# A feed-forward whose gate/up pairs go by Strassen's scheme in a two-block network kernel

## The reference

```python
D_MODEL = 1024; SEQ = 512; DEPTH = 2; D_FF = 2816

def rms_norm(x, w):
    y = xf * lax.rsqrt(jnp.mean(xf * xf, axis=-1, keepdims=True) + NORM_EPS)
    return (y * w.astype(jnp.float32)).astype(x.dtype)

def swiglu_ffn(x, w_gate, w_up, w_down):
    return (jax.nn.silu(x @ w_gate) * (x @ w_up)) @ w_down

for l in range(DEPTH):
    x = x + 0.5 * swiglu_ffn(rms_norm(x, ffn1_norm_w[l]), ffn1_w_gate[l], ffn1_w_up[l], ffn1_w_down[l])
    x = x + hybrid_mixer(rms_norm(x, mix_norm_w[l]), ...)
    x = x + 0.5 * swiglu_ffn(rms_norm(x, ffn2_norm_w[l]), ffn2_w_gate[l], ffn2_w_up[l], ffn2_w_down[l])
```

## Time and profile before

| | us |
|---|---|
| median of 3 runs | 3319.2 (3318.94 to 3319.91) |
| span of the profiled execution | 3318.2 |
| TensorE busy | 3261.9 |
| VectorE busy | 1223.7 |
| ScalarE busy | 1229.1 |
| GpSimd busy | 1382.5 |

### The profile page before, as it was taken

One profiled execution on the slowest core, in us unless ns is written; L12 is line 12 of the kernel. 1 busy time (PEld: TensorE's weight loads), 2 busy tenths in 40 slices (PEclk: granted clock), 3 DMA queues, 4 the chain that ended last, 5 costly groups with the idle time before them and its releaser, 6 DMA issues.

```text
span 3318.2 us, 40330 instructions
## 1 busy us (share of the span) xinstructions
PE 3261.9 (98%) x16417; PEld 2646.5 (80%) x16417; DVE 1223.7 (37%) x2060; ACT 1229.1 (37%) x1830; POOL 1382.5 (42%) x614
## 2 busy tenths in 40 slices
PE   8999999999999999999999999999999999999998
PEld 6888877788888888877788887778866796878887
DVE  4220476432203220386432205743455434542211
ACT  4322445432314222445443314521366452343322
POOL 5444532354445444532354445553211242434442
PEclk9999999999999999999999999999999999999999
DMA  5332321233323332321233323238233432223332
...
DMA packets 470469, 305.99 MB, mean 92 GB/s; under 512 B 68840, under 2 KB 441944, under 8 KB 470284
## 3 DMA queue, kind: packets, MB, share of 16 engines
...
## 4 chain that ended last, share of the span: by engine, by line
PE 86%; DVE 9%; ACT 2%; DVEq 1%; issue 1%; DMA 0%; SPq 0%; POOL 0%; ACTq 0%
PE ps L545 37%; PE ps L563 13%; PE ps L3175 5%; PE ps L959 3%; PE ps L2852 3%; PE ps L1303 3%; PE ps L2497 3%; PE ps L1531 2%; PE ps L1311 2%; DVE h_lo L392 1%; PE ps L3153 1%; PE ps L798 1%; PE ps L2176 1%; PE ps L2864 1%; PE ps L2896 1%; PE ps L2874 1%
## 5 line engine op out<-in xcount | busy, mean ns | idle before, releaser
L179 POOL TENSOR_TENSOR w_lo<-w_raw,w_hi 128x1024 fp32r<-128x1024 f32 x518 | 1279.2, 2472 | 1891.1 <-ACT w_hi L171 1890.3
L171 ACT ACTIVATE w_hi<-w_raw 128x1024 fp32r<-128x1024 f32 x518 | 543.8, 1054 | 1001.7 <-PE ps L545 354.6
L545 PE MATMUL ps<-h_hi,w_hi 128*128 128x512 f32 x1952 | 768.1, 393 | 7.0 <-DVE h_lo L392 4.3
L545 PE MATMUL ps<-h_hi,w_lo 128*128 128x512 f32 x1952 | 760.4, 390 | 0.0
L545 PE MATMUL ps<-h_lo,w_hi 128*128 128x512 f32 x1952 | 760.3, 390 | 0.0
L545 PEld LDWEIGHTS ps<-h_hi,w_hi 128*128 128x128 f32 x1952 | 366.8, 188 | 89.9 <-issue 7.0
L545 PEld LDWEIGHTS ps<-h_lo,w_hi 128*128 128x128 f32 x1952 | 366.9, 188 | 78.2 <-issue 3.4
L545 PEld LDWEIGHTS ps<-h_hi,w_lo 128*128 128x128 f32 x1952 | 366.9, 188 | 77.1
L563 PE MATMUL ps<-a_hi,w_hi 128*128 128x512 f32 x640 | 249.0, 389 | 0.0
L563 PE MATMUL ps<-a_lo,w_hi 128*128 128x512 f32 x640 | 249.0, 389 | 0.0
L563 PE MATMUL ps<-a_hi,w_lo 128*128 128x512 f32 x640 | 249.0, 389 | 0.0
...
## 6 DMA issues: line engine op xcount, KB each, us to landing
w_raw<-in_w_in_dram SPq DMA_DIRECT2D x128, 512.0 KB, 3.8
...
```

The lines of the kernel that those rows point to most:

```text
L171: act.activation(self.hi[:, s, :, :], self.raw[:, s, :, :], ACT.Copy).then_inc(self.halved[s], 1)
L179: pool.tensor_tensor(self.lo[:, s, :, :], self.raw[:, s, :, :], self.hi[:, s, :, :].bitcast(F32), ALU.subtract)\
L545: mm = pe.matmul(out, w, (c.h_hi, c.h_lo)[low][:, k, :], start=(k == 0 and i == 0), stop=(k == KD - 1 and i == 2))
```

## The change

KF and the tiles stay. The first WHOLE = 2 pairs are made as before. For the other N = 20, the 1024 rows of weight are cut into two halves of 4 chunks, and the tokens into an early and a late half of 256. Gate and up of a pair are then a product of 2x2 blocks, which Strassen's scheme (in Winograd's form) makes with seven block products in place of eight: `first`, `second`, ... `seventh`, each 4 chunks x 3 passes = 12 matmuls of 256 columns.

The scheme needs sums of its operands. Once in a feed-forward, in its head, ScalarE makes a plain `h` (eight activations) and VectorE four sums of 128x1024 of it (`sum`, `s_plain`); ScalarE and VectorE split them into `s_hi` and `s_lo`, and the one called `sum` into the late half of `h_hi` and `h_lo`. Once in a pair, VectorE makes four sums of 128x512 of the raw weights (`pair_first`, two in `pair_second`, `pair_seventh`); ScalarE rounds them and one raw half (`pair_high`), and GpSimd makes three of the rests and that of the raw half (`pair_low`), VectorE the fourth (`second_low`). The up tile no longer goes through `high_to` and `low_to`; the gate tile does. A slot is loaded again only when the sums that read it are made as well (`read_too`).

Partial products are added while they leave PSUM: ScalarE copies the first (`keep`, 128x256), and VectorE adds (`m.second`, `m.third`, late and early up, late gate, each 128x256). TensorE waits for some of these before it adds the next product into the same bank. The products `a` of silu and up stay plain in `a_rows`; `a_hi` and `a_lo` are now rings of A_RING = 6 rows in the place of `s_hi` and `s_lo`, filled during the down product (`row_high`, `row_low`). The transposes of the last feed-forward use banks 3 and 7 (two in place of four), and the down product opens bank 3 first.

```diff
-def ffn(nc, c, acc, scale, g, finish=None, turns=None, late_sum=False):
+WHOLE = 2
...
+        self.a_hi = nc.alloc_sbuf_tensor_at(f"a_hi_{nc.next_id()}", [P, A_RING, SEQ], F32R, offset=s_at)
...
+        def row_high(act, j):
+            if j < KF:
+                act.wait_ge(c.product.sem, pb + j + 1)
+                if j >= A_RING:
+                    w.wait_used(act, t0 + 2 * KF + j - A_RING)
+                act.activation(m.a_hi[:, j % A_RING, :], m.a[:, j, :], ACT.Copy).then_inc(c.a_high.sem, 1)
...
+            def product(out, w_hi, w_lo, x_hi, x_lo, opens):
+                for k in range(KH):
+                    for i, (wt, x) in enumerate(((w_hi, x_hi), (w_hi, x_lo), (w_lo, x_hi))):
+                        mm = pe.matmul(out, wt[:, k, :], x(k), start=(opens and k == 0 and i == 0), stop=(k == KH - 1 and i == 2),
+                                       skip_group_check=True)
...
+            def sixth(n):
+                pe.wait_ge(c.second_low.sem, sb + n + 1)
+                product(bank(n, 1), m.t_hi[:, 0], m.t_lo[:, 0], of_mix(m.s_hi, 0), of_mix(m.s_lo, 0), True).then_inc(c.partial.sem, 1)
...
+            def seventh(n):
+                pe.wait_ge(*spread_at(n, SECOND))
+                pe.wait_ge(c.pair_low.sem, qb + 3 * n + 2)
+                product(bank(n, 1), m.t_hi[:, 1], m.t_lo[:, 1], of_mix(m.s_hi, 1), of_mix(m.s_lo, 1), False).then_inc(c.partial.sem, 1)
...
+            for n in range(N):
...
+                sixth(n)
...
+                fifth(n)
+                second(n)
+                seventh(n)
+                third(n)
+                if n < N - 1:
+                    first(n + 1)
+                fourth_product(n)
...
+            def pair_high(n):
+                t = up_tile(n)
+                act.wait_ge(c.pair_made.sem, tb + 4 * n + 1)
+                act.activation(high(t, 0), first_sum(n), ACT.Copy).then_inc(c.pair_high.sem, 1)
+                act.wait_ge(c.pair_made.sem, tb + 4 * n + 2)
+                act.activation(m.t_hi[:, 0], m.t_plain[:, 0], ACT.Copy).then_inc(c.pair_high.sem, 1)
+                w.wait_loaded(act, t)
+                act.activation(high(t, 1), raw(t, 1), ACT.Copy).then_inc(w.halved[t % SLOTS], 1)
+                f = fourth(n)
+                act.wait_ge(c.pair_made.sem, tb + 4 * n + 3)
+                act.activation(m.t_hi[:, f], m.t_plain[:, f], ACT.Copy).then_inc(c.pair_high.sem, 1)
+                act.wait_ge(c.pair_made.sem, tb + 4 * n + 4)
+                act.activation(m.t_hi[:, 1], m.t_plain[:, 1], ACT.Copy).then_inc(c.pair_high.sem, 1)
...
+            def keep(n):
+                act.wait_ge(c.partial.sem, xb + 1 + (5 * (n - 1) + NEXT1 if n else 0))
+                if n >= 2:
+                    act.wait_ge(*spread_at(n - 2, GATE2))
+                act.activation(m.first[:, n % 2, :], bank(n, 0), ACT.Copy).then_inc(c.first_kept.sem, 1)
...
+            for k in range(KD):
+                ins = act.activation(m.h[:, k, :], c.x_T[:, k, :], ACT.Copy, scale=c.gains[:, own, k:k + 1])
+            ins.then_inc(c.h_scaled.sem, 1)
...
+            def pair_low(n):
+                t = up_tile(n)
+                pool.wait_ge(c.pair_made.sem, tb + 4 * n + 2)
+                pool.wait_ge(c.pair_high.sem, jb + 4 * n + 1)
+                pool.tensor_tensor(low(t, 0), first_sum(n), high(t, 0).bitcast(F32), ALU.subtract).then_inc(c.pair_low.sem, 1)
+                pool.wait_ge(w.halved[t % SLOTS], t // SLOTS + 1)
+                pool.tensor_tensor(low(t, 1), raw(t, 1), high(t, 1).bitcast(F32), ALU.subtract).then_inc(w.split[t % SLOTS], 1)
+                for i, made in ((1, 4), (fourth(n), 3)):
+                    pool.wait_ge(c.pair_high.sem, jb + 4 * n + made)
+                    pool.tensor_tensor(m.t_lo[:, i], m.t_plain[:, i], m.t_hi[:, i].bitcast(F32), ALU.subtract).then_inc(c.pair_low.sem, 1)
...
+            def mix_low(i, made):
+                dve.wait_ge(c.mix_high.sem, ib + made)
+                dve.tensor_tensor(m.s_lo[:, i], m.s_plain[:, i], m.s_hi[:, i].bitcast(F32), ALU.subtract).then_inc(c.mix_low.sem, 1)
...
+            def pair_first(n):
...
+                dve.tensor_tensor(first_sum(n), raw(up_tile(n), 0), raw(gate_tile(n), 0), ALU.subtract).then_inc(c.pair_made.sem, 1)
+
+            def pair_second(n):
+                dve.drain()
+                dve.tensor_tensor(m.t_plain[:, 0], raw(up_tile(n), 1), first_sum(n), ALU.subtract).then_inc(c.pair_made.sem, 1)
+                dve.drain()
+                dve.tensor_tensor(m.t_plain[:, fourth(n)], raw(gate_tile(n), 1), m.t_plain[:, 0], ALU.subtract).then_inc(c.pair_made.sem, 1)
+
+            def pair_seventh(n):
+                t = up_tile(n)
+                dve.tensor_tensor(m.t_plain[:, 1], raw(t, 1), raw(t, 0), ALU.subtract).then_inc(c.pair_made.sem, 1)
+
+            def second_low(n):
+                dve.wait_ge(c.pair_high.sem, jb + 4 * n + 2)
+                dve.tensor_tensor(m.t_lo[:, 0], m.t_plain[:, 0], m.t_hi[:, 0].bitcast(F32), ALU.subtract).then_inc(c.second_low.sem, 1)
+
+            def second_gate(n):
+                p = (WHOLE + n) % 2
+                dve.wait_ge(*last_at(n))
+                dve.tensor_tensor(gt[:, p, LATE], bank(n, 1), m.first[:, n % 2, :], ALU.add)
+                dve.drain()
+                dve.tensor_tensor(gt[:, p, LATE], gt[:, p, LATE], c.rstd[:, LATE], ALU.mult).then_inc(c.spread.sem, 1)
...
+            dve.wait_ge(c.h_scaled.sem, c.h_scaled.n + 1)
+            dve.tensor_tensor(m.sum[:, :, :], m.h[:, 0:KH, LATE], m.h[:, KH:KD, LATE], ALU.add).then_inc(c.mix_made.sem, 1)
+            dve.drain()
+            dve.tensor_tensor(m.s_plain[:, 0], m.sum[:, :, :], m.h[:, 0:KH, EARLY], ALU.subtract).then_inc(c.mix_made.sem, 1)
+            dve.drain()
...
+            gate_whole(0)
+            mix_low(0, 1)
+            mix_low(2, 2)
+            mix_low(1, 3)
+            up_whole(0)
...
+            up_whole(1)
+            dve.wait_ge(c.mix_high.sem, ib + 4)
+            dve.tensor_tensor(c.h_lo[:, 0:KH, LATE], m.sum[:, :, :], c.h_hi[:, 0:KH, LATE].bitcast(F32), ALU.subtract)\
...
+            for n in range(N):
+                p = (WHOLE + n) % 2
+                if n:
+                    second_gate(n - 1)
+                if n < N - 1:
+                    pair_first(n + 1)
+                dve.wait_ge(*partial_at(n, SUM2))
+                dve.wait_ge(c.first_kept.sem, fb + n + 1)
+                dve.tensor_tensor(m.second, bank(n, 1), m.first[:, n % 2, :], ALU.add).then_inc(c.spread.sem, 1)
+                if n < N - 1:
+                    pair_second(n + 1)
+                dve.wait_ge(*partial_at(n, SUM5))
+                dve.tensor_tensor(m.third, bank(n, 2), m.first[:, n % 2, :], ALU.add).then_inc(c.spread.sem, 1)
+                if n < N - 1:
+                    second_low(n + 1)
+                multiply(WHOLE + n - 1)
+                w.wait_used(dve, gate_tile(n))
+                dve.tensor_tensor(gt[:, p, EARLY], bank(n, 0), c.rstd[:, EARLY], ALU.mult).then_inc(c.spread.sem, 1)
+                dve.wait_ge(*partial_at(n, SUM7))
+                dve.drain()
+                dve.tensor_tensor(up[:, p, LATE], bank(n, 1), m.third, ALU.add).then_inc(c.spread.sem, 1)
+                if n < N - 1:
+                    pair_seventh(n + 1)
+                w.wait_used(dve, up_tile(n))
+                dve.tensor_tensor(up[:, p, EARLY], bank(n, 2), m.second, ALU.add).then_inc(c.spread.sem, 1)
+                dve.drain()
+                dve.tensor_tensor(up[:, p, :], up[:, p, :], c.rstd[:, :], ALU.mult)
+            second_gate(N - 1)
...
+            def row_low(j):
+                dve.wait_ge(c.a_high.sem, hb + j + 1)
+                dve.tensor_tensor(m.a_lo[:, j % A_RING, :], m.a[:, j, :], m.a_hi[:, j % A_RING, :].bitcast(F32), ALU.subtract)\
...
-            for i in range(KF):
-                p = i % 2
...
+            for j in range(A_RING):
+                row_low(j)
```

More of the change, by code:

```diff
@@ L638, in ffn, with pairs_read @@
+def pairs_read(c, t0):
+    for n in range(KF - WHOLE):
+        t = t0 + 2 * (WHOLE + n)
+        c.w.read_too[t] = c.pair_made.at(4 * n + 3)
+        c.w.read_too[t + 1] = c.pair_made.at(4 * n + 4)
+def ffn(nc, c, acc, scale, own, g, finish=None, turns=None, late_sum=False):
     w = c.w
     a = c.arena
+    ps = c.ps
     t0 = w.take(3 * KF)
+    N = KF - WHOLE
     with a.scope():
-        a_hi, a_lo = a.sb("a_hi", [P, KF, SEQ], F32R), a.sb("a_lo", [P, KF, SEQ], F32R)
-        both = a.sb("both", [P, 4, SEQ])
@@ new lines, in bank, with raw, high, low @@
+        def bank(n, x):
+            return ps[:, (4, 0)[n % 2] + x, 0:HALF]
+        def raw(t, half):
+            return w.raw[:, t % SLOTS, KH * half:KH * half + KH, :]
+        def high(t, half):
+            return w.hi[:, t % SLOTS, KH * half:KH * half + KH, :]
+        def low(t, half):
+            return w.lo[:, t % SLOTS, KH * half:KH * half + KH, :]
+        def first_sum(n):
```

(30 more changed lines are left out.)

277 lines of the change are left out of this document (203 added, 74 removed).

## The result

The changed kernel takes **3600.4 us** (median of 4 runs, 3599.5 to 3602.2), the kernel before 3319.1 (4 runs): 1.0848 times as long, 95% interval 1.0836 to 1.0861. The forecast was 3549 with a range of 3390 to 3650. The profiled execution spans 3598.4 us, so 280 more than before, against a forecast of +230.

What follows compares the result with a forecast made beforehand. TensorE, busy 98% of the span, bounds the kernel. Five feed-forwards of +45.4 us (-16.1 matmuls, +9.6 and +4.4 head, +18 x 2.46 pairs, +3.2 tail), +6.5 first, -3 last: +230, so 3549 us, range 3390 to 3650.

Steps and rivals of the forecast that it cites:

- TensorE's own part: In a pair, 84 matmuls of 256 columns replace 48 of 512: 10.08 us for 10.89, saving 16.1 us a feed-forward.
- The step on contention: In a pair, VectorE instructions with two SBUF inputs and GpSimd instructions wait for each other, costing VectorE 5.1 us.
- VectorE without idle time in a pair: A sign to look for in the trace: VectorE's queue is never idle within a steady pair.
- 12.54: Average time in us forecast for a steady pair, 2.46 above TensorE's 10.08, counted 18 times a feed-forward.
- the open cost: TensorE's clock falling at the head's stalls: 0 to 3 us a feed-forward, taken as 0.
- a rival put aside because the mixers have idle pieces too: Short idle pieces in pairs bring TensorE to 1.2 GHz; a tenth of pairs gives 3620; chance 0.1, shared with late loads.
- The head: Start of each feed-forward: TensorE stalls 9.6 us before the first `sixth`, and the first pair takes 14.5 us for 10.1.
- the transposes fall into TensorE's waits, some 3 us less: In the last feed-forward, eight groups of transposes run while TensorE would wait anyway, saving some 3 us.
- The start of the sum: Time of a feed-forward up to its down product before the change, counted at 240.3 us.
- Meeting less: Rival: GpSimd works mostly beside VectorE's PSUM instructions, drains and idle moments; pair 10.8 to 11.5 us, whole 3365 to 3430; chance 0.11.
- Faster, without contention: Rival: VectorE's raw weight sums and GpSimd do not wait for each other; pair 10.08 us, whole 3282; chance 0.09.
- The break-even pair of 10.5 us: Pair time at which the change turns from loss to gain, if the head has no waits for GpSimd.

Runs made afterwards that it cites:

- e1: Changed kernel with seven of VectorE's eight two-SBUF-input instructions given an input in PSUM in pairs 1 to 19, computing other numbers; 3354.0 us.
- e2: Changed kernel with GpSimd's four rests of a pair made over 128 of their 512 columns, computing other numbers; 3369.1 us.
- e6: Changed kernel with five intermediate sums in PSUM, VectorE's queue reordered and four whole tiles in place of two before the first Strassen pair; 3310.8 us.
- e4: Changed kernel with 12 extra matmuls (the fill) before TensorE's wait at `third`, pairs 1 to 19 of the first four feed-forwards; 3583.3 us.
- e7: Changed kernel with only VectorE's queue in another order, all eight instructions with two SBUF inputs kept; 3557.9 us.
- e9: e6 with the whole tiles of its head in more PSUM banks, same result; 3289.1 us, ratio 0.9911 to the kernel before.

## Why the forecast held, and where it was off

**Sign and mechanism.** TensorE's own part is right: its 256-column matmuls start 0.12 us apart, and e1's pair of 10.20 is near the 10.08. The step on contention is right, from both sides (e1, e2). Places and sizes, as mean less the undisturbed duration (0.68, or 0.42 for 256 columns): `pair_first` 1.43 us (forecast 1.1), the two sums of `pair_second` 0.89 and 1.13, together 2.0 (1.7), `second_low` 0.71 (0.75), the late gate's scaling 0.40 (0.5), the multiply 0.03 (1.1). Together, with the seventh sum and the up scaling, 4.7 us for 5.1. The multiply was wrong: by then GpSimd is done, since the waits ahead of it took longer. Wrong too was the sign "VectorE without idle time in a pair": it idles 0.66 us, so the pair is 7.5 + 4.7 + 0.7 = 12.9 us. That 12.54 came so near is in part luck: waits 0.4 too long stood against idle time that was put at nothing.

**Where TensorE waits.** Forecast: 2.5 us, first at `third`, then at `fourth_product`, about 1 us each. Measured: all of it at `third`, 1.9 us; the late up half is made in time since the multiply does not wait.

**Size.** +281 for +230. The missing 51 us, by the starts of TensorE's matmuls:
- The pairs. From the first `sixth` of the second pair to that of the last, 18 distances, a pair takes 12.97 us for 12.54 (the 12.89 above is of VectorE's rows, over 17 distances): 0.43 x 18 x 5 = 39 us. The clock is 0.27 of it (in the four feed-forwards with the fill 12.71 for 12.98), some 24 us if the fifth is like them; the other 15 are the layout. This is the step that was mis-sized: the open cost "0 to 3 us a feed-forward; I take 0", and for the pairs a rival put aside because the mixers have idle pieces too. The rows that I had the earlier trace rows were of a stretch with 3.2 us idle in 10; here one idle piece of 1.9 to 2.4 us in 35 of 90 pairs brought slow rows.
- The head. The first pair took 16.3 us (15.9 to 17.0) for 14.5, since its products ran at half speed: 1.8 x 5 = 9 us.
```profile
756.00:766.00 10.00, 7.22 (x37) 6.92 (x37) 7.83 (x9) 5.21 (x8) 7.12 (x5) 0.55 0.16 48
```
  The first `sixth` comes 33.0 us after the start of the three middle feed-forwards (forecast 33.7), behind two stalls (in the second 3.1 for the gate tile's `w_lo` and 4.5 for `second_low`, the late `h_lo` then 2.8), and in the first 2 us less late than laid out: 4 us too much in all.
- The last feed-forward: "the transposes fall into TensorE's waits, some 3 us less" was wrong. Before, it was 4.7 us longer than the middle ones up to the down product (245.9 and 241.2), and now it is 6.2 longer (300.9 and 294.7). Nothing was saved, and its `sixth` is 0.8 late on top: 4 us too little.
- The start of the sum: a feed-forward up to its down product was counted at 240.3 us, and the trace before has 241.2. That is 0.9 x 5 = 4.5 us too much.
- The down product: its part was put at nothing, and in the first feed-forward it is 119.5 us, as before. In the next three it is 121.2 and in the last 122.4, with its first rows at half speed behind the tail's stall: 8 us. In e6 three of five were 119.6. So the halves made there cost nothing, and the clock behind the stall does. The stall itself is 3.05 us a tail (forecast 3.2).

39 + 9 - 4 + 4 - 4.5 + 8 is the missing 51. Slow rows are behind some 41 of it (24, 9 and 8, an estimate from these differences), and only the 24 have an experiment of their own (e4).

**The rivals.** Meeting less: not seen in the changed kernel, and e7 shows that another order of the same work gives only 12.5. Faster, without contention: e1 is that case for the pair, and gives 3354, not 3282. The forecast had 2.6 and 3.0 us of stall for the head and 1.8 for the tail in that case; the traces show e1 with the head's three stalls still at 56 us over the five, nearly as many as with contention (58). The break-even pair of 10.5 us, reckoned for a head without waits for GpSimd, was thus too high. With the head mended and a pair of 10.2 the sign does turn (e9).
